# A decoder block on eight cores: the stages from convolution to FFN run per half of the tokens

## The reference

```python
h = rms_norm(x, norm_mix); z = h @ w_in          # q, k, v of three branches, gates, u
o_nsa = gated sum of compressed, selected and window attention   # 8 heads, (B,T,1024)
o_conv = conformer_conv(u, ...)                   # GLU, causal depthwise conv of 31 taps,
                                                  # LayerNorm over 1024 channels, silu
x = x + concatenate([o_nsa, o_conv]) @ w_out
# memory cross-attention, 4 heads of 128 over 256 memory tokens
hq, hm = rms_norm(x, norm_mem_q), rms_norm(mem, norm_mem_kv)
q = rms_norm(hq @ w_mq); k = rms_norm(hm @ w_mk); v = hm @ w_mv
x = x + (softmax(q k^T / sqrt(128)) v) @ w_mo
h3 = rms_norm(x, norm_ffn)
x = x + (silu(h3 @ w_gate) * (h3 @ w_up)) @ w_down
```

## Time and profile before

| what | value |
|---|---|
| median of 3 runs | 1968.61 us (1966.34 to 2040.44) |
| the profiled execution | 1968.34 us, span of its slowest core (core 1) 1966.9 us |
| spans of the other cores | 1953.6 to 1965.2 us |
| TensorE busy | 1747.5 us (89%) |
| VectorE / ScalarE / GpSimd busy | 774.6 / 519.0 / 157.8 us |
| weight loads (GpSimd queue) | 107.13 MB written, 41.7% of the DMA engines' span |

### The profile page before, as it was taken

How to read it: one execution, slowest core, us unless ns; L and a number is a source line. 1 busy time by engine, 2 the same in 40 slices (tenths; PEclk the granted TensorE clock), 3 DMA queues, 4 the chain that set the end, 5 groups by cost and what they waited for, 6 DMA issues and landing times.

```text
span 1966.9 us, 30326 instructions; the slowest of 8 cores (1953.6 to 1966.9 us)
## 1 busy us (share of the span) xinstructions
PE 1747.5 (89%) x10960; PEld 958.2 (49%) x10960; DVE 774.6 (39%) x1555; ACT 519.0 (26%) x912; POOL 157.8 (8%) x145
## 2 busy tenths in 40 slices
PE   2799998999996727995768999999999999999999
PEld 1466645666663206883334444444444444444444
DVE  3344113566665452225473414144141432514324
ACT  2334244778776442004431000000000000000000
POOL 1100100000001411000000010010100001000000
PEclk9899998999997868996888999999999999999999
DMA  9821877413417317941221192663917539185454
GB/s 211 148 86 44 98 77 90 77 40 50 77 32 136 89 57 198 145 66 22 43 43 17 27 129 35 94 87 42 129 25 105 80 50 129 16 114 70 60 86 171
DMA packets 196753, 162.00 MB, mean 82 GB/s; under 512 B 14336, under 2 KB 185984, under 8 KB 192256
## 3 DMA queue, kind: packets, MB, share of 16 engines
q0 software_dynamic: 173968, 107.13, 41.7%
q1 hardware_dynamic: 22640, 52.93, 8.6%
HBM read 249.79 MB, written 8.52 MB: 131 GB/s over the span
## 4 chain that ended last, share of the span: by engine, by line
PE 79%; DVE 5%; DMA 5%; another core or an unknown queue 4%; issue 3%; ACT 3%; POOL 1%; SPq 0%; DVEq 0%; ACTq 0%; POOLq 0%
PE pair L1269 16%; PE bank L1271 15%; PE pair L1286 8%; PE bank L1286 8%; PE pair L521 5%; PE bank L521 4%; DMA arena<-sel 4%; PE pair L1142 3%; PE bank L1142 3%; PE pair L831 2%; PE bank L676 2%; PE bank L810 2%; PE bank L681 2%; PE pair L528 2%
## 5 line engine op out<-in xcount | busy, mean ns | idle before, releaser
L1269 PE MATMUL pair<-arena 128*128 128x512 bf16 x1408 | 319.7, 380 | 0.0
L1271 PE MATMUL bank<-arena 128*128 128x512 bf16 x1408 | 318.3, 379 | 0.0
L1274 DVE TENSOR_TENSOR arena<-bank,arena 128x512 bf16<-128x512 f32 x88 | 60.9, 692 | 548.3 <-PE pair L1269 442.8
L1273 ACT ACTIVATE arena<-pair 128x512 bf16<-128x512 f32 x88 | 52.6, 598 | 823.9 <-PE pair L1269 804.1
L820 ACT ACTIVATE arena<-bank,arena 128x512 bf16<-128x512 f32 (+3 forms) x402 | 215.2, 576 | 76.3 <-PE pair L831 30.2
L1269 PEld LDWEIGHTS pair<-arena 128*128 128x128 bf16 x1408 | 138.2, 98 | 167.0 <-issue 1.9
L1271 PEld LDWEIGHTS bank<-arena 128*128 128x128 bf16 x1408 | 137.7, 98 | 166.2
L1286 PE MATMUL pair<-arena 128*128 128x512 bf16 x704 | 168.1, 379 | 0.0
L1286 PE MATMUL bank<-arena 128*128 128x512 bf16 x704 | 166.3, 379 | 0.0
L469 PE MATMUL bank<-arena 128*128 128x128 bf16 x544 | 52.5, 273 | 116.6 <-DVE arena L461 116.6
L831 PE MATMUL pair<-arena 128*128 128x129 bf16 (+1 forms) x1184 | 123.6, 224 | 23.4 <-DVE arena L824 21.2
(11 more groups left out here) (174 smaller groups left out, 1717.6 us busy)
## 6 DMA issues: line engine op xcount, KB each, us to landing
arena<-xc SPq DMA_DIRECT2D x24, 1024.0 KB, 9.6
arena<-w_gate POOLq DMA_DIRECT2D x22, 1024.0 KB, 11.3
arena<-w_up POOLq DMA_DIRECT2D x22, 1024.0 KB, 12.8
arena<-w_down POOLq DMA_DIRECT2D x22, 1024.0 KB, 12.6
arena<-w_in POOLq DMA_DIRECT2D x18, 1024.0 KB, 12.5
arena<-arena SPq DMA_DIRECT2D x64, 135.0 KB, 2.5
arena<-w_out POOLq DMA_DIRECT2D x8, 1024.0 KB, 32.6
y<-arena SPq DMA_DIRECT2D x8, 1024.0 KB, 4.0
```

The costliest lines, as they stand in the source:

```text
L1269: op(PE, lambda: nc.tensor.matmul(bank[pg][:, :], lhsT=wgt[:, kc, cc * 128:(cc + 1) * 128], rhs=h3T[:, kc, tc * 512:(tc + 1) * 512], start ...
L1271: op(PE, lambda: nc.tensor.matmul(bank[pu][:, :], lhsT=wut[:, kc, cc * 128:(cc + 1) * 128], rhs=h3T[:, kc, tc * 512:(tc + 1) * 512], start ...
```

## The change

The kernel after computes the same. What is different:

- *Fences.* Each buffer belongs to the scope that was last allocated from; closing a scope records, for each of its byte ranges, the last accesses of its buffers. A new tile waits for the recorded accesses to the ranges that it overlaps, and for no others. `free` is gone.
- *Convolution.* The tensor of its results is split into one per half. The memory rows are loaded at the stage's start, and the norm of their two tiles is put between groups 1 and 6. The statistics of both halves use banks 4 and 5.
- *Residual rows* are two tensors of four token tiles. Half 0 is loaded behind the convolution, half 1 behind the LayerNorm chunks of half 1, which stand behind the memory keys and values.
- *Output projection.* Half 0 goes through all 8 weight blocks; blocks 0 and 1 are then given back, 2 to 7 are held. Half 1 uses 2 to 7 and loads 1 and 0 a second time. The two blocks of `w_mq` are loaded once for each half, too.
- *Weaving.* `weave(main, filler)` emits the steps of one generator and, wherever the modelled clocks say that the next step isn't ready, single matmuls of the other. In this order: norm, query projection and attention of half 0 with the output projection of half 1; norm of half 1 with the memory output projection of half 0; FFN norm of half 0 with the query projection of half 1; attention of half 1 with the first gate/up block of half 0; FFN norm of half 1 with the memory output projection of half 1 and the second gate/up block of half 0. Norms of half 1 scale on ScalarE (`by_act`), and attention's division has two small VectorE steps fewer per head.
- *FFN.* The loop begins with what is left of its first two blocks; the two down blocks of these are loaded behind them. The stores stand inside the last pass.

```diff
     def close(self):
+        toks = {}
+        for b in self.bufs:
+            for t in list(b.w.values()) + list(b.r.values()):
+                _add(toks, t)
         for off, n in self.blocks:
             self.K.arena_release(off, n)
-        self.blocks = []
+            self.K.history.append((off, off + n, toks))
+        self.blocks, self.bufs = [], []
...
+        b = Buf(name, self.fence)
+        if self.cur_scope is not None:
+            self.cur_scope.bufs.append(b)
+        self.fence_used = True
+        return b
...
+        if self.fence_used:
+            self.fence, self.fence_used = {}, False
+        self.cur_scope = S
+        for a, b, toks in self.history:
+            if a < o + nb and o < b:
+                for t in toks.values():
+                    _add(self.fence, t)
...
+        self.wo_at = len(self.wq)
         for i in range(8):
+            self.wq.append((wcol(self.w_out, 256 * i), (16, 256)))
+        for i in range(2):
+            self.wq.append((wcol(self.w_mq, 256 * i), (16, 256)))
+        for i in (1, 0):
             self.wq.append((wcol(self.w_out, 256 * i), (16, 256)))
         for i in range(2):
             self.wq.append((wcol(self.w_mq, 256 * i), (16, 256)))
         for i in range(2):
             self.wq.append((wrow(self.w_mo, 256 * i), (2, 2048)))
...
+        qgate(0)
+        qgate(1)
+        qdown(0)
+        qdown(1)
+        for j in range(2, 22):
+            qgate(j)
+            qdown(j)
...
+        def weave(main, filler):
+            sync_clocks()
+            for t in main:
+                while t > PE.clk and next(filler, self) is not self:
+                    pass
+
...
+        def norm_half(N, gcol, dst, dstb, by_act=False, gate=None):
...
+                op(ACT, lambda: nc.scalar.activation(out=xs[i % 2][:, :], in_=x3(i), func=AF.Square, accum_out=s_[:, 0:1]), r=xbufs(i), w=[xsb[i % 2], sb_])
...
+            for i in range(n):
+                if by_act:
+                    op(ACT, lambda: nc.scalar.activation(out=xs[i % 2][:, :], in_=x3(i), func=AF.Copy, scale=ss[i % 2][:, 2:3]), r=list(xbufs(i)) + [ssb[i % 2]], w=[xsb[i % 2]])
+                else:
+                    yield need([ssb[i % 2]])
+                    op(DVE, lambda: nc.vector.tensor_scalar(out=xs[i % 2][:, :], in0=x3(i), scalar1=ss[i % 2][:, 2:3], scalar2=None, op0=ALU.mult), r=list(xbufs(i)) + [ssb[i % 2]], w=[xsb[i % 2]])
+                yield from gated(i + 1)
+                if i + 1 < n:
+                    stat(i + 1)
+                for half in range(2):
+                    yield need([xsb[i % 2]], [bankb[rot_tr.peek()]])
+                    bi = rot_tr.next()
+                    bv = bank[bi][:, :].bitcast(BF16)
+                    for c8 in range(8):
...
-        cv = self.tile(CV, "cv", [128, 8, TQ], F32)
...
+        for k in range(8):
+            conv_group(k)
+            if k in (1, 4):
+                norm_tile_a(mt_[0][:, :], [mtb[0]], mxs, mxsb, mss, mssb)
+                if k == 1:
+                    dma(SP, mt_[0][:, :], self.memb[128:256, :], w=[mtb[0]])
+            if k in (3, 6):
+                norm_tile_b(PV_NMKV, hmT, 128 * (k // 6), hmTb, mxs, mxsb)
+        while pend:
+            pend.pop(0)()
+        SM.close()
...
+        cv[1] = self.tile(CV[1], "cv1", [128, 8, 512], F32)
+        cvb_[1] = [self.buf(f"cv1_{c}") for c in range(8)]
+        ln_prep()
+        for k in range(8, 16):
+            conv_group(k)
+            ln_chunk(0, k - 8)
+        while pend:
+            pend.pop(0)()
+        CV[0].close()
+        HG.close()
...
+        xr_load(0)
+
+        self.mark("memkv")
+        ln_prep()
...
+        ln_step(8)
+        HM.close()
+        CM.close()
+        CV[1].close()
+
+        xr_load(1)
...
+        def w_out_block(cb, wt, wb, h, rot):
+            for tt in range(4):
...
+                    yield True
+                dst = xr[h][:, tt, cb * 256:(cb + 1) * 256]
+                op(DVE, lambda: nc.vector.tensor_tensor(out=dst, in0=bank[psi][:, 0:256], in1=dst, op=ALU.add), r=[bankb[psi]], w=[xrb[h][tt][cb]])
...
+        wo = {}
         for cb in range(8):
             wt, wb = wget()
...
+            wo[cb] = (self.wcur - 1, wt, wb)
+            drain(w_out_block(cb, wt, wb, 0, rot_proj))
+            if cb < 2:
+                wdone(wo[cb][0])
+
+        def w_out_second():
+            for cb in (2, 3, 4, 5, 6, 7, 1, 0):
+                if cb < 2:
+                    i = self.wo_at + 11 - cb
+                    wo[cb] = (i,) + wtake(i)
+                i, wt, wb = wo[cb]
+                yield from w_out_block(cb, wt, wb, 1, rot_f)
+                wdone(i)
...
+        def mq(h, hb, hbb):
+            for blk in range(2):
+                i = self.wo_at + (8, 12)[h] + blk
+                while not wready(i):
+                    yield PE.clk + 1.0
+                wt, wb = wtake(i)
+                for cc in range(2):
+                    hd = blk * 2 + cc
+                    yield need([hbb, wb], [bankb[rot_m.peek()]])
+                    psi = rot_m.next()
...
+                        if h == 1:
+                            yield 0.0
+                    flush(0)
+                    pnorm(psi, 512, eps[:, 3:4], [epsb], qmnT[:, hd, :], qmnTb[hd])
+                wdone(i)
+            yield need([sqtb[rot_sq.i % 2 ^ 1]])
+            flush(0)
...
+            for tt in range(4):
+                for cb4 in range(4):
+                    psi = rot_f4.next()
...
+                    dst = xr[h][:, tt, cb4 * 512:(cb4 + 1) * 512]
+                    op(DVE, lambda: nc.vector.tensor_tensor(out=dst, in0=bank[psi][:, :], in1=dst, op=ALU.add), r=[bankb[psi]], w=[xrb[h][tt][2 * cb4], xrb[h][tt][2 * cb4 + 1]])
+                self.mo_rows[h] = tt + 1
...
+        f2 = w_out_second()
+        weave(chain(norm_half(N0, PV_NMQ, HB[0], HBb[0]), mq(0, HB[0], HBb[0]), mattn(0)), f2)
+        drain(f2)
...
+        for j in (1, 2):
+            HB[j] = self.tile(M0, f"HB{j}", [128, 16, 512], BF16)
+            HBb[j] = self.buf(f"HB{j}")
+        N1 = (xrow(1)[0], xrow(1)[1]) + N0[2:]
+        f3 = mo(0)
+        weave(norm_half(N1, PV_NMQ, HB[1], HBb[1], by_act=True), f3)
+        drain(f3)
...
+        def glu_first(jb):
+            while len(wgu) <= jb:
...
+            _, (wgt, wgb_), _, (wut, wub) = wgu[jb]
             for cc in range(2):
...
+
+        f6 = mq(1, HB[1], HBb[1])
+        weave(norm_half(N0, PV_NFFN, HB[2], HBb[2]), f6)
+        drain(f6)
...
+        f4 = glu_first(0)
+        weave(mattn(1), f4)
+        drain(f4)
+        def mo_glu():
+            yield from mo(1)
+            for i, _, _ in wmo:
+                wdone(i)
+            yield from glu_first(1)
+
+        f5 = mo_glu()
+        weave(norm_half(N1, PV_NFFN, HB[0], HBb[0], by_act=True, gate=lambda i: self.mo_rows[1] > i), f5)
+        drain(f5)
...
-            wrel(2, newest=True)
-            wdt, wdb = wget()
-            dheld.append((aj, wdt, wdb))
+                for tc in range(1 if jb < 2 else 0, 2):
```

497 lines of the change are left out of this document (265 added, 232 removed).

## The result

The changed kernel takes 1904.56 us (median of 4 runs, 1900.99 to 1907.24) against 1968.0 for the kernel before beside it: a ratio of 0.968, with a 95% interval of 0.966 to 0.970. (All times are medians of the executions in the faster of two states; in the other, which every kernel falls into now and then, the cores of a die get a lower granted clock and the time is some per cent longer, as the 2040.44 us of one run of the kernel before.) It is 63 us faster, where the prediction said 94; the time lies in the predicted range, 31 us above the forecast of 1874. The profiled execution has its slowest core in core 1 again, span 1903.6 us. First the windows by stage; columns as in the earlier trace rows, to which they answer.

The account below looks back on a forecast made before the run. The prediction took chains of small steps with no other work beside them as the bound. Its stage terms from 646 us summed to 1226.3 against 1320.6, 94.3 saved, giving 1874 us, range 1849 to 1917.

Parts of the forecast that it names:

- Chains without cover are the bound: Between 646 and 1049 us: small steps with no other work beside them, some 150 us of empty TensorE at most.
- Attention 0: Attention before 646 us: the finer fence waits for the same instruction, so no change; bounds -3.5 to +1 us.
- keys and values 17.5: LayerNorm of half 1 and memory keys/values: 58.1 us before, 17.5 after, bounds 14 to 20.
- projections 61 and 87: Output projection: half 0 in 61 us (56 work, +5); half 1 with norm, query, attention in 87 (81 work, +6).
- FFN 888.3: FFN loop: 917.9 us less 27.6 of moved gate/up work and 2 for the cold start.
- The 2 us for the cold start of the FFN: FFN loop: 2 us taken off its time for the cold start.
- Convolution 73: Convolution with the memory norm's steps in its first half: 66.2 us before, 73 after; +7, bounds 0 to +14.
- The four stages behind the projections, 99.5: From the projections to the FFN loop: 88.5 us of work plus 11 of stalls, bounds +3 to +25.
- (a): First projection half: late weights bound it, 28 us in place of 5, total time 1897 us; chance 0.12.
- (b): Woven stages: TensorE is committed to work that isn't ready, 38 us for 12, total time 1900 us; chance 0.11.
- (c): Output projection to FFN: many short waits keep the clock at 1.2 GHz, total time about 2099 us; chance 0.04.
- (d): Woven norms: VectorE's scaling holds up weight loads, 12.8 us, total time 1887 us; chance 0.03.

Follow-up runs that it names:

- e6: Changed kernel with every weave from the second projection half on undone, all filler matmuls first: 1974.3 us.
- e7: Changed kernel, but a new tile waits for the last accesses of every closed scope, as a global fence does: 1909.9 us.
- e4: Changed kernel without the memory norm, its result a constant: 1890.7 us.
- e11: Changed kernel without GpSimd's products for the convolution from the third group on: 1892.8 us.
- e1: Changed kernel, but between the first w_mq and second FFN up load, weight loads may overtake one whose slot is still held: 1885.5 us.
- e2: Changed kernel with four PSUM banks instead of two for the query projection of half 1: 1895.6 us.
- e13: Changed kernel, but VectorE's bf16 copy of the convolution's result is made from the PSUM bank, bias added: 1902.8 us.

## Why the prediction was right in sign and 30 us off in size

- *Chains without cover are the bound, and weaving removes them:* right, and shown by e6, which undoes only that. Its worth, 70 us, is more than the whole gain.
- *Attention 0, keys and values 17.5, projections 61 and 87, FFN 888.3:* right within 1.1 us each. In the first projection half the one wait is for VectorE, 4.7 against "about 5". Weights cost nothing there, but by little: blocks 4 to 7 land 0.9 to 6.0 us before they are wanted (3 to 8 in the prediction), and the wait for VectorE is part of that margin. The second half is right in sum rather than term by term: VectorE costs 3.9 of the 5 and query weights none of the 1, while 1.1 us are the start of the wait for `w_mo` and 1.8 are busy time above the counted work. The 0 for attention was not put to a test, since the start of the convolution lies 14 us apart by core. The 2 us for the cold start of the FFN stand in no row; in the kernel before its first 16 matmuls take 5.08 us, the next 3.62. The finer fences were costed for attention alone, at nothing; e7 puts 5 to 8 us on them in the projections.
- *Convolution 73, measured 79.8:* the mechanism was right, the size not, though it lay within the bounds. The term took the scaling and copies from rows of a stretch where GpSimd is idle. In the convolution GpSimd builds the taps' products, and the rows of the kernel before at 678 and 685 us show there what these do to VectorE; e4 and e11 put the norm at 7 to 11 us without them and 13 with them. The sum also counted waits alone, and not that TensorE works on at half clock behind each.
- *The four stages behind the projections, 99.5, measured 121.9:* this step failed. Its +11 counted VectorE, the last evacuation and banks of the gate/up blocks. It left out that the queue issues in order, so that `w_mo` stood behind two `w_mq` loads whose slots the filler still held (12 us, e1), and that the second query projection has two banks (4.4 us, e2). About 5 more there, the uncovered ends of the norm of half 1 and of the FFN norm, are read from waits only. Nor did it have a term for the lower clock behind the waits; some 7 of the missing 22 are TensorE's busy time beyond the 88.5 of work, part of them within the 12 of e1.
- *Rivals.* (a) fell: no weight wait in the first half on core 1, 0.5 us on cores 5 and 6. e7 and the landing of block 4 show that the supply has no slack. (b) happened in one place: TensorE was committed to `w_mo` before it was there; 12 us, not 26. (c) fell: clock 0.97 and 0.98 in the projections, 0.84 to 1.00 behind them. (d) fell for weights: beside woven scalings no load made TensorE wait in the second projection half. The lock itself is real; it was weighed against the DMA issues and not against GpSimd's own work in the convolution, 100 us earlier.

## What to carry to other kernels

When a stage is woven into another, price each moved step with the engines that will run beside it, GpSimd and VectorE above all, and follow every load in an in-order queue back to the release that the load ahead of it waits for. Chains cut into more and shorter pieces cost more when alone (their ends, and the half clock behind them), so a split pays only with a filler. Before taking a wait away, look what lies under it: here a 4.7 us wait for VectorE hid weights that landed 0.9 us before they were wanted.

## What the hardware showed that was not expected

- GpSimd's product and VectorE's operations from SBUF take turns: the copy 0.43 to 2.13 us, the scaling 1.28 to 1.85 (2.08 in e13), the product 1.91 to 2.92, an fp32 step with two inputs 0.69 to 2.40 (kernel before) and 2.22 (changed kernel, e13). The copy with its input in PSUM, 0.74 or 0.75, showed no such spread, as the Trainium skill's rule (VectorE: DVE Perf Modes, section "Why PSUM operands drop a tier") would have it: the mode that takes both SBUF read ports is closed to an operand in PSUM.
- The part before the convolution, in which only fences changed, ends between 632.9 and 647.1 us by core in the changed kernel and between 634.9 and 646.3 in the kernel before, late on other cores in other executions; why stays open. The slowest core is often the one that drew the late start, which is one reason why totals differ by more than the stages do.
